# Query start of the expert stage, per token tile: last projection, second norm, head 0's query and scores for tile 0 ahead of tile 1

## What is computed

```python
merged = jax.nn.sigmoid(g_conv) * conv_out + jax.nn.sigmoid(g_attn) * attn_out
x = x + merged @ w_out[l]
h2 = rmsnorm(x, norm2_g[l])
x = x + peer(h2, w_peer_q[l], peer_sub_keys[l], peer_u[l], peer_v[l])

def peer(h, w_pq, sub_keys, u_emb, v_emb):
    q = (h @ w_pq).reshape(B, S, PEER_HEADS, 2, PEER_DHALF)      # 8 heads, two halves of 128
    sc = jnp.einsum("bshcd,hcnd->bshcn", q, sub_keys)            # 128 keys for each half
    s_top, i_top = lax.top_k(sc, PEER_TOPK)                      # 16 of each half
    cand = s_top[..., 0, :, None] + s_top[..., 1, None, :]       # 16 x 16 sums
    best, pos = lax.top_k(cand, PEER_TOPK)                       # 16 experts for each head and token
    # gate = softmax(best); out = sum over the 128 chosen experts of
    # gate * gelu(u_emb[expert] . h) * v_emb[expert]
```

## Time and profile before

| | us |
|---|---|
| median of 3 runs | 1798.57 (1798.48 to 1799.08) |
| the profiled execution | 1801.52 |
| its span | 1799.5 |
| busy: PE, DVE, ACT, POOL | 1514.9, 972.8, 567.5, 305.5 |
| first gather issued | 359.40 |
| mean granted clock of TensorE | 0.950 |

### The profile page before, as it was taken

The page is one execution under the profiler, slowest core; times in us unless marked ns, Lnnn a source line. Parts: engine busy times, 40 slices in busy tenths (PEclk is TensorE's granted clock), DMA queues, the critical chain, the costliest instruction groups (busy, mean ns, idle before and its releaser), DMA issues.

```text
span 1799.5 us, 18415 instructions
## 1 busy us (share of the span) xinstructions
PE 1514.9 (84%) x7014; PEld 1077.3 (60%) x7014; DVE 972.8 (54%) x1922; ACT 567.5 (32%) x1197; POOL 305.5 (17%) x296
## 2 busy tenths in 40 slices
PE   7999699879977776777777769886999969879997
PEld 5768586555433232323332259663999869559996
DVE  2896521375567676767765553323455454345554
ACT  1001520132333333333333234441333334323333
POOL 2000000033344344344444200300000000000000
PEclk9999899989999999999999989898999979989999
DMA  9964013399999999999999914123344424135551
GB/s 256 198 214 152 1 47 141 126 408 386 389 421 420 419 420 416 411 420 419 408 409 420 398 48 173 53 94 140 130 179 176 177 111 153 63 125 188 188 187 47
DMA packets 52023, 428.69 MB, mean 238 GB/s; under 512 B 6880, under 2 KB 7032, under 8 KB 9824
## 3 DMA queue, kind: packets, MB, share of 16 engines
q0 software_dynamic: 40720, 279.20, 40.1%
q1 hardware_dynamic: 11216, 148.33, 21.7%
HBM read 422.50 MB, written 4.98 MB: 238 GB/s over the span
## 4 chain that ended last, share of the span: by engine, by line
PE 63%; DMA 19%; DVE 10%; ACT 5%; issue 2%; POOL 0%; DVEq 0%; SPq 0%; ACTq 0%; POOLq 0%
PE psum L595 21%; DMA pool<-uv,experts 17%; PE psum L813 10%; PE psum L686 9%; PE psum L687 9%; PE psum L688 9%; DVE pool L1473 3%; PE psum L628 2%; PE psum L644 2%; DMA ring<-stream 1%; DVE w_lo L1263 1%; ACT L1097 1%; ACT diag L1107 1%; ACT xn L904 1%; DVE hT L1198 1%
## 5 line engine op out<-in xcount | busy, mean ns | idle before, releaser
L813 PE MATMUL psum<-pool,diag 128*128 128x512 f32 x1024 | 489.1, 628 | 151.7 <-ACT diag L1107 141.9
L813 PEld LDWEIGHTS psum<-pool,diag 128*128 128x128 f32 x1024 | 195.4, 199 | 441.3 <-ACT diag L1107 223.0
L1473 DVE CUSTOM_DVE_ANT_0 pool<-pool,xn 128x1024 f32<-128x1024 f32 x256 | 313.8, 1226 | 216.5 <-DMA pool<-uv,experts 215.2
L552 POOL DMA_INDIRECT pool<-uv,experts x256 | 273.6, 1069 | 714.7 <-PE psum L813 371.7
L1263 DVE TENSOR_TENSOR w_lo<-ring,w_hi 128x2048 fp32r<-128x2048 f32 x86 | 196.8, 2292 | 218.2 <-ACT w_hi L961 218.2
L961 ACT ACTIVATE w_hi<-ring 128x2048 fp32r<-128x2048 f32 x86 | 164.3, 1914 | 326.4 <-PE psum L688 326.4
L686 PE MATMUL psum<-h_hi,w_hi 128*128 128x256 f32 x704 | 201.6, 286 | 22.4 <-DVE h_lo L1274 22.4
L687 PE MATMUL psum<-h_lo,w_hi 128*128 128x256 f32 x704 | 201.1, 286 | 0.0
L688 PE MATMUL psum<-h_hi,w_lo 128*128 128x256 f32 x704 | 201.1, 286 | 0.0
L595 PE MATMUL psum<-hT,ring 128*128 128x256 f32 x768 | 171.2, 385 | 5.4 <-DMA ring<-stream 2.8
L595 PEld LDWEIGHTS psum<-hT,ring 128*128 128x128 f32 x768 | 148.2, 193 | 28.8 <-issue 5.1
(11 more groups left out here) (214 smaller groups left out, 1858.8 us busy)
## 6 DMA issues: line engine op xcount, KB each, us to landing
ring<-stream SPq DMA_DIRECT2D x66, 2048.0 KB, 7.5
pool<-uv,experts POOLq DMA_INDIRECT x256, 12.6
ring<-stream SPq DMA_DIRECT2D x3, 1024.0 KB, 6.0
t_scratch<-att POOLq DMA_DIRECT2D x1, 2048.0 KB, 92.8
rpb_scratch<-att POOLq DMA_DIRECT2D x7, 256.0 KB, 28.7
ring<-stream SPq DMA_DIRECT2D x1, 1792.0 KB, 8.1
row<-rows POOLq DMA_DIRECT2D x1, 1672.0 KB, 15.4
ring<-stream SPq DMA_DIRECT2D x1, 1664.0 KB, 6.8
```

The lines of the kernel that those rows point to most:

```text
L552: gp.indirect_dma_start(out=gath[:, n % NROWS, :], out_offset=None, in_=uv, in_offset=bass.IndirectOffsetOnAxis(ap=experts[:, n:n + 1], ax ...
L813: last = nc.tensor.matmul(psum[:, RB + half, :], diag[:, n % NDIAG, :], gath[:, n % NROWS, D + 512 * half:D + 512 * half + 512], start=k = ...
L1473: ins = V.tensor_tensor_reduce(out=row_u, in0=row_u, in1=xn[:, n // SLOTS, :], scale=1.0, scalar=0.0, op0=ALU.mult, op1=ALU.add, accum_out ...
```

## The change

The four parts of the output projection run in the order (0,0), (1,0), (0,1), then, behind tile 0's norm, query and scores, (1,1). The transposes, query of head 0 (`pq0`) and scores of head 0 (`sc0`) are made for each tile on its own: a tile's query is 16 matmuls of 128 columns instead of half of 16 matmuls of 256, its scores are two matmuls. ACT takes the roots and these copies tile by tile. DVE adds part (0,1), does the whole selection of unit 0, and only then adds part (1,1) and norms tile 1; the selection of unit 1 follows. `QUERY_ORDER` starts with `pq 1, pq 2, sc 1` and `EARLY_QUERIES` is 5 instead of 7, so that the same work as before stands ahead of the expert stage. The list of fills grows by two, which shifts the bank of every later fill.

```diff
-QUERY_ORDER = [("pq", 0), ("sc", 0), ("pq", 1), ("pq", 2), ("sc", 1)]
+QUERY_ORDER = [("pq", 1), ("pq", 2), ("sc", 1)]
...
-EARLY_QUERIES = 7
+EARLY_QUERIES = 5
...
-    out += fm_fills("convout", 2) + fm_fills("attno", 2) + tm_fills("wout", 2)
-    out += norm_fills("N2")
+    out += fm_fills("convout", 2) + fm_fills("attno", 2)
+    out += [("wout", 0, 0), ("wout", 1, 0), ("wout", 0, 1), ("N2", 0, 0), ("N2", 0, 1), ("pq0", 0), ("sc0", 0)]
+    out += [("wout", 1, 1), ("N2", 1, 0), ("N2", 1, 1), ("pq0", 1), ("sc0", 1)]
...
+            def second_norm(t):
+                pe.wait_ge(xn_ready, xn_before["N2"] + t + 1)
+                for hf in range(2):
+                    transposes(("N2", t, hf), [xn[:, t, P * k:P * k + P] for k in range(4 * hf, 4 * hf + 4)])
+                for hf in range(2):
+                    wait_emptied(pe, ("N2", t, hf))
+
+            def first_query(t):
+                w = wait_chunk(pe, ("pq", 0))[:, 0:4096].rearrange("p (k n) -> p k n", k=KD)
+                dst = begin(("pq0", t))
+                for c in range(2):
+                    last = accumulate(dst[:, P * c:P * c + P],
+                                      [(w[:, k, P * c:P * c + P], hT[:, k, tile128(t)]) for k in range(KD)])
+                last.then_inc(bank_filled, 1)
+                wait_emptied(pe, ("pq0", t))
+                dst = begin(("sc0", t))
+                for c in range(2):
+                    last = nc.tensor.matmul(dst[:, NKEYS * c:NKEYS * c + NKEYS], qpT[:, 0, c, tile128(t)],
+                                            keys[:, c, :], start=True, stop=True)
+                last.then_inc(bank_filled, 1)
+
+            out_projection(0, 0)
+            out_projection(1, 0)
+            out_projection(0, 1)
             pe.wait_ge(keys_landed, 16)
+            second_norm(0)
+            first_query(0)
+            out_projection(1, 1)
+            second_norm(1)
+            first_query(1)
...
-            norm_roots(sums("wout"))
+            def first_query_copies(t):
+                empty(("pq0", t), qpT[:, 0, :, tile128(t)], lambda b: b[:, 0:S].rearrange("p (c n) -> p c n", c=2))
+                empty(("sc0", t), scores[:, t, 0:2 * NKEYS], lambda b: b[:, 0:2 * NKEYS])
+
+            for t in range(NT):
+                for i in range(2):
+                    wait_emptied(act, ("wout", i, t))
+                root(x[:, t, :], xn[:, t, :], ssq[:, t:t + 1], t, D)
+                first_query_copies(t)
...
-                        wait_emptied(dve, ("sc", head))
+                        wait_emptied(dve, ("sc", head) if head else ("sc0", t))
...
-            for unit in range(2):
-                for k in range(SELECT_STEPS):
-                    select_step(unit, k)
+            add_tile(0, 0)
+            add_tile(1, 0)
+            second_norm(0)
+            add_tile(0, 1)
+            for k in range(SELECT_STEPS):
+                select_step(0, k)
+            add_tile(1, 1)
+            second_norm(1)
+            for k in range(SELECT_STEPS):
+                select_step(1, k)
```

More of the change, by code:

```diff
@@ L156 @@
 assert len(FILL_NO) == len(FILLS)
-LAST_USE = {("pq", 0): ("pq", 1), ("pq", 1): ("pq", 3), ("pq", 2): ("pq", 5), ("pq", 3): ("pq", 7), ("kpe_uq", 0): ("uqa", 0, 1), ("uq_ukv", 0): ("ukv", 1, 1),
+LAST_USE = {("pq", 0): ("pq", 1), ("wout", 0): ("wout", 0, 1), ("pq", 1): ("pq", 3), ("pq", 2): ("pq", 5), ("pq", 3): ("pq", 7), ("kpe_uq", 0): ("uqa", 0, 1), ("uq_ukv", 0): ("ukv", 1, 1),
             ("ws", 0): ("gating", 1)}
@@ L777, in _, with out_projection @@
             pe.wait_ge(merged_ready, 1)
-            token_major_chunks("wout", 2, hT)
-            norm_transposes("N2", xn)
-            pe.wait_ge(keys_landed, 16)
+            def out_projection(i, t):
+                w = wait_chunk(pe, ("wout", i))[:, 0:4096].rearrange("p (k n) -> p k n", k=KD)
+                dst = begin(("wout", i, t))
+                accumulate(dst, [(hT[:, k, tile128(t)], w[:, k, :]) for k in range(KD)]).then_inc(bank_filled, 1)
+            def second_norm(t):
[20 more added lines that the diff above has]
+            out_projection(0, 1)
+            pe.wait_ge(keys_landed, 16)
+            second_norm(0)
[3 more added lines that the diff above has]
+            first_query(1)
             def query(kind, head):
@@ L1069, in _ @@
             attention(att1)
-            norm_roots(sums("wout"))
+            def first_query_copies(t):
[6 more added lines that the diff above has]
+                first_query_copies(t)
             def query_copy(kind, head):
                 if kind == "pq":
-                    if head >= 2:
+                    if head == 2:
+                        act.wait_ge(bank_filled, FILL_NO[("sc0", 1)] + 1)
+                    elif head > 2:
                         act.wait_ge(bank_filled, FILL_NO[("sc", head - 2)] + 1)
@@ L1409, in _, with add_tile, second_norm @@
             V.tensor_tensor(hT[:, :, :], sgc, sga, ALU.add).then_inc(merged_ready, 1)
-            add_to_x("wout")
-            normed("N2", rows_=row_("norm2"))
-            gained("N2", hT)
+            def add_tile(i, t):
+                b = wait_filled(dve, ("wout", i, t))
+                d = x[:, t, 512 * i:512 * i + 512]
+                V.tensor_tensor(d, d, b, ALU.add).then_inc(emptied_sem(("wout", i, t)), 1)
+            def second_norm(t):
+                dve.wait_ge(root_ready, roots_before["N2"] + t + 1)
+                r = rstd[:, t:t + 1]
+                link(V.reciprocal(r, r))
+                V.scalar_tensor_tensor(xn[:, t, :], x[:, t, :], r, row_("norm2"), ALU.mult, ALU.mult).then_inc(xn_ready, 1)
+                for hf in range(2):
+                    b = wait_filled(dve, ("N2", t, hf)).rearrange("p (k n) -> p k n", k=4)
+                    V.tensor_copy(hT[:, 4 * hf:4 * hf + 4, tile128(t)], b).then_inc(emptied_sem(("N2", t, hf)), 1)
             def top16(src, values, indices):
```

## The result

The changed kernel takes 1811.05 us in the median of five runs (1806.90 to 1811.58), the kernel before 1798.57 (1795.11 to 1800.80). The medians differ by 12.5 us; the ratio, by which the kernels are compared from here on, is 1.0056, 95% interval 1.0041 to 1.0070, which is +10.1 us (+7.4 to +12.6): slower, as forecast, and by more than the forecast +7.5, which lies just inside the interval. The profiled execution has a span of 1809.6 us, 10.1 above the one before.

The account below looks back on a forecast made before the run. Until 497 us PE and DVE, through head 1's scores and the first dot product, were taken to bound the kernel, though DMA looks full. Scores 6.1 us later plus 1.4 clock gave +7.5 on 1798.57: 1806.1 us, range 1801.5 to 1811.

Parts of the forecast that it names:

- Step 1: Reordered projection: 6.87 us a part, tile 0's xn ready near 323.8, hidden behind PE's third part until 325.65.
- Step 2: Tile 0's transposes, query (4.0 us) and scores: selection 0 starts at 333.3, first gather 15.4 us earlier, near 344.
- Step 3: PE ends part (1,1) at 339.8 and waits, as DVE adds it only behind selection 0, at 343.15.
- Step 4: Tile 1's xn at 346.9, then transposes, query and copy: head 1's scores start at 368.0, 6.1 us later.
- Step 5: Slow PE clock after the 7.1 us stop before tile 1's transposes: costs 1.4 us, ends 0.5 and 4.0.
- Step 6: Everything behind head 1's scores keeps its distances, later by the same amount; ninth gather near 392, early gathers' head start lost.
- B: PE stays at half clock beyond tile 1's query into head 1's: 1810 to 1813 us; chance 0.09.
- C: Gather stage goes by its bytes, so the shift mostly vanishes: 1800.5 to 1803.5 us, centre 1802; chance 0.13.
- D: DVE paces the first units and its 12.4 us idle before dot products goes: faster, 1793.7 us; chance 0.08.

Follow-up runs that it names:

- e11: Changed kernel with eight unread matmuls filling PE's stop and the first gather held back until tile 1's scores of head 0 are filled; ratio to before 1.0025.
- e7: Changed kernel with the first gather held back on POOL until tile 1's scores of head 0 are filled; ratio to before 1.0056.
- e12: e8 with the first step of the third selection moved behind the second dot product; ratio to before 0.9967.
- e3: Kernel before with the scores of head 1 made ahead of the query of head 2; ratio to before 1.0004.
- e8: Changed kernel, part (1,1) behind tile 0's transposes, tile 1 normed before selection 0, scores of head 1 ahead of query 2; ratio to before 0.9960.
- e9: Changed kernel, part (1,1) behind tile 0's transposes, tile 1 normed before selection 0, query order as in the changed kernel; ratio to before 0.9983.
- e4: Changed kernel with the scores of head 1 made ahead of the query of head 2; ratio to before 1.0042.
- e10: e4 with the first step of the third selection moved behind the second dot product; ratio to before 1.0016.
- e1: Changed kernel with part (1,1)'s addition and tile 1's norm on DVE ahead of selection 0; ratio to before 1.0029.
- e2: Changed kernel with tile 1's addition and norm put between the steps of selection 0; ratio to before 1.0038.
- e5: Changed kernel with the edits of e2 and e4 together; ratio to before 1.0020.
- e6: Changed kernel with eight unread 128x512 matmuls on PE between part (1,1) and tile 1's transposes; ratio to before 1.0042.

## Why the prediction was right

The way and the mechanism held: the wait of PE behind selection 0 delays head 1's scores, and this passes on to the end. The range of 1801.5 to 1811.0 holds by the ratio (1798.57 x 1.0056 = 1808.6); the median itself, 1811.05, lies 0.05 us above it. The centre was 2.6 us low by the ratio.

1. Step 1, the norm of tile 0 hidden: it ended at 323.67 by the timeline (322.39 + 1.28), before PE was through with part (0,1). Right. Unforeseen was that the projection started at the full clock in the profile of after, which brought the second addition 14.0 us after the first matmul instead of 15.6. That the absolute times of the forecast came so close (selection 0 at 332.77 for 333.3, the first gather at 343.43 for 344) is in part luck: this profile's start, later by 1.4 us, and its faster projection, by 1.6, cancel.
2. Step 2: the query of a tile was forecast at 4.0 us and took 3.81; the copy of 0.38 was right.
3. Step 3, the wait: PE's stop was forecast at 7.1 us and is 7.16, released by xn.
4. Step 4: from the addition to the end of xn 3.76 us were forecast and measured (342.52 to 346.28).
5. Step 5, the clock, is the term that was mis-sized: 1.4 us, against 3.1 by e11. I took the length of the slow stretch, 3.3 to 4.6 us, from two restarts into matmuls of 512 columns, and counted it from the restart. Here the clock fell 2.5 us before the restart at 346.34 and came back 7.7 us after it, behind the transposes, a pause and nearly the whole query. The case of the upper bound of 4.0 (all of the query at half speed) is nearly the one that came. Nor were the two restarts the whole of the scatter: ahead of the expert matmuls, after stops of 6.2 to 9.9 us, the clock came back 2.9 to 6.2 us after the restart in 12 profiles, while after tile 1's transposes began it took 6.6 to 7.7 us in all seven profiles with the stop. The Trainium skill (TensorE: Matmul & The Clock Gate, What's actually happening) names a stretch of time and not a number of matmuls, from which I had drawn that thin work at a restart is as good as dense work. The traces don't bear this out: the seven restarts with thin work all took longer than the twelve others, though not twice as long as the slowest of these. That the thin work is the reason is not shown.
6. Step 6, the distances: first dot to first expert matmul 6.65 us in both; ninth gather forecast at 392, came at 392.43; the DMA share from 370 to 390 was forecast well under one half and was near 0.4; the chain went over to DMA at 505.94, forecast 504. That the early gathers are worth nothing is shown by e7.

With the same start of the projection on both sides head 1's scores were forecast 7.5 us late and are 8.6 late; 1.7 of the difference is the clock, and the two shorter queries give 0.4 back. Behind them the profile adds 0.6 us in the gather stage and 1.1 behind it, where nothing was edited; the stretch behind the last gather is between 776.3 and 778.8 in the 14 profiles without an order by kernel. So I take this rest for scatter, which the runs' own spread (4.7 us after, 5.7 before) bears out but does not prove.

Of the rivals, B (a slow clock beyond tile 1's query, into that of head 1) did not come: the clock was back at 354.1, 1.2 us before tile 1's query ended, and the block of 64 records behind it took 13.82 us as before. C, the stage going by its bytes, falls with e7: bytes moved 14 us later change nothing. D wanted the idle time of DVE before its dot products, 12.4 us up to 420, to go. It did not go, though the first eight rows had long landed. The same group after, over the stretch moved by 8 us (288 to 428):

```profile
L1526 DVE CUSTOM_DVE_ANT_0 pool<-pool,xn 128x1024 f32<-128x1024 f32 x19 | 23.0, 1224 | 12.2 <-DMA pool<-uv,experts 12.1
```

The first eight dot products no longer wait for rows, and from the ninth on, whose gather starts only at 392.43, the others wait as long in sum. In e12 the rows are the limit, so C was a rule of a faster kernel and not of this one.

Left open: what of e3's 2 us of earlier expert matmuls was lost. Its last gather is 2.9 us earlier by the profile, its time is unchanged by the runs, within 0.1%. The profile of e3 is that of its fastest run, 1796.29 us against a median of 1800.99, so its timeline may flatter it.

## What to carry to other kernels

Before work is split so that a transfer can start earlier, ask which wait opens the stage behind it. Here eight buffers filled early and then stood full, because their first reader depended on scores that the split had pushed behind a new wait of PE. Splitting by tile paid only when the pieces of one tile were laid into the waits of the other (e8, e9), and after each gate that fell the next stood close behind: head 1's scores, head 2's scores, then the rows. Put a small piece of work that many wait for, such as an addition of 0.7 us, ahead of a long one on the same engine, not behind it. And before two profiles are subtracted, look whether the restarts ahead of the change ran at the same clock in both: here one did and one didn't, which hid 1.6 us of the cost.

## What the runs showed of the hardware

- After the stop of 7.16 us ahead of tile 1's transposes (changed, e4, e7, e10) TensorE's granted clock was 0.50 for 10.2 us, the last 7.6 to 7.7 of them at work. After stops of 3.9 and 4.8 us (e1, e2, e5) it was 0.50 for 6.8 us. In e1 it fell only 0.7 us after PE had started again, and the query took 6.38 us instead of 3.81.
- A stop of 3.2 us ahead of the projection was followed by 3.4 us at 0.50 in 7 of 14 profiles and by none in the others, with the same code; it costs 1.6 us where it comes. In e3 even the stop of 2.2 us ahead of the transposes was followed by it (331.0 to 334.4), in the kernel before it was not. With e6's matmuls in the stop the clock stayed at 1.00.
- 32 records of 128 columns took 3.81 us at the full clock, 0.12 us each, and 7.14 us for 256 columns: half the columns cost 53%, so splitting a float32 product by tile costs little.
- ACT's copy came 2.7 us late with the DMA engines full of rows (e6) and on time without (e11). That it waited for its own instructions is inferred.
